# Expert biases of a mixture-of-experts layer: one-hot bias products on TensorE against rows loaded per block and copied into PSUM by VectorE

## The reference, cut to what matters

```
logits = x2d @ w_router + b_router
top_v, top_e = lax.top_k(logits, 4);  gates = softmax(top_v)
# the 2080 (token, expert) slots are sorted by expert and cut into blocks of one expert each
def expert_block(xb, e):
    hh = xb @ w_up[e] + b_up[e]                      # 2048 wide
    gate = minimum(hh[:, :1024], 7);  lin = clip(hh[:, 1024:], -7, 7)
    return (gate * sigmoid(1.702 * gate) * (lin + 1)) @ w_down[e] + b_down[e]
y[token] += gates * expert_block(...)
```

## Time and profile before

| | |
|---|---|
| median of the runs | 1387.74 us |
| span of the profiled execution | 1384.6 us |
| TensorE busy | 1333.6 us (96%) |
| VectorE busy | 927.2 us (67%) |
| ScalarE, GpSimd busy | 199.2 us, 108.2 us |
| DMA | 468.77 MB, mean 339 GB/s over the span |
| product groups of the loop | L1874 639.5 us, L1909 319.5 us |

### The profile page before, as it was taken

How to read it: one execution, slowest core, us unless ns; L and a number is a source line. 1 busy time by engine, 2 the same in 40 slices (tenths; PEclk the granted TensorE clock), 3 DMA queues, 4 the chain that set the end, 5 groups by cost and what they waited for, 6 DMA issues and landing times.

```text
span 1384.6 us, 22327 instructions
## 1 busy us (share of the span) xinstructions
PE 1333.6 (96%) x6750; PEld 546.0 (39%) x6750; DVE 927.2 (67%) x2107; ACT 199.2 (14%) x389; POOL 108.2 (8%) x152
## 2 busy tenths in 40 slices
PE   8999999988998999998999999899999998999997
PEld 7866565553332333332333333233333332333332
DVE  3525257655876777776687776677787775777778
ACT  4231133422010100100010100000010000000012
POOL 3000000000000001000100001000100000000100
PEclk9999989999999999999999999999999999999999
DMA  9505171055999999999999999999999999999995
GB/s 362 120 4 185 31 251 69 31 231 207 393 421 421 421 383 421 391 421 421 422 379 420 389 422 421 419 420 380 421 392 413 396 420 422 420 378 422 388 379 236
DMA packets 90653, 468.77 MB, mean 339 GB/s; under 512 B 11822, under 2 KB 28960, under 8 KB 40226
## 3 DMA queue, kind: packets, MB, share of 16 engines
q1 hardware_dynamic: 74318, 441.43, 78.8%
q0 software_dynamic: 7360, 16.79, 3.1%
q10 hardware_dynamic: 8948, 10.19, 2.1%
HBM read 623.60 MB, written 28.25 MB: 471 GB/s over the span
## 4 chain that ended last, share of the span: by engine, by line
PE 86%; DMA 9%; DVE 4%; issue 1%; ACT 0%; SPq 0%; DVEq 0%
PE ps L1874 42%; PE ps L1909 21%; DMA raw<-in_w_down_dram 8%; PE ps L1542 5%; PE ps L1565 5%; PE ps L1781 4%; PE ps L1844 2%; PE ps L1736 1%; PE ps L1735 1%; PE ps L1830 1%; PE ps L1520 1%; DVE v_gate L1481 0%; PE ps L1644 0%; PE ps L1727 0%; DVE v_gate L1475 0%
## 5 line engine op out<-in xcount | busy, mean ns | idle before, releaser
L1874 PE MATMUL ps<-raw,xT 128*64 128x512 f32 x2880 | 639.5, 594 | 14.3 <-DMA raw<-in_w_up_dram 14.1
L1874 PEld LDWEIGHTS ps<-raw,xT 128*64 128x64 f32 x2880 | 201.2, 137 | 388.6 <-issue 348.3
L1909 PE MATMUL ps<-raw,aT 128*64 128x512 f32 x1440 | 319.5, 593 | 7.9 <-DMA raw<-in_w_down_dram 7.9
L1370 DVE STREAM_TRANSPOSE xT<-x_hold 32x64 f32<-32x64 f32 (+1 forms) x704 | 282.5, 401 | 57.1 <-PE ps L1874 36.5
L1370 DVE STREAM_TRANSPOSE aT<-act_g 32x256 f32<-32x256 f32 x360 | 228.6, 635 | 54.6 <-PE ps L1909 44.4
L1909 PEld LDWEIGHTS ps<-raw,aT 128*64 128x64 f32 x1440 | 102.0, 137 | 210.1 <-issue 185.8
L874 ACT ACTIVATE act_s<-act_g 128x512 f32<-128x512 f32 x46 | 29.0, 630 | 714.2 <-DVE act_g L1354 714.1
L516 POOL DMA_INDIRECT slot_outputs<-y_rows,out_idx x44 | 44.4, 1010 | 603.4 <-ACT y_rows L879 603.4
L1276 DVE TENSOR_REDUCE found<-ps 128x2 f32<-128x8 f32 x48 | 8.0, 167 | 109.3 <-PE ps L1830 107.3
L508 POOL DMA_INDIRECT x_rows<-expert_inputs,row_idx x48 | 49.3, 1028 | 345.1 <-DVE row_idx L1277 209.7
L1781 PE MATMUL ps<-w_out_sb,mixT 128*128 128x512 f32 x128 | 56.8, 598 | 0.8 <-DVE mixT L1154 0.8
(11 more groups left out here) (368 smaller groups left out, 894.8 us busy)
## 6 DMA issues: line engine op xcount, KB each, us to landing
raw<-in_w_up_dram SPq DMA_DIRECT2D x368, 1024.0 KB
raw<-in_w_down_dram SPq DMA_DIRECT2D x184, 1024.0 KB
slot_outputs<-zeros ACTq DMA_DIRECT2D x1, 8320.0 KB, 28.1
raw<-slot_outputs SPq DMA_DIRECT2D x8, 1024.0 KB, 11.9
w_c_cols<-in_w_in_dram SPq DMA_DIRECT2D x1, 4096.0 KB, 32.0
w_out_sb<-in_w_out_dram SPq DMA_DIRECT2D x1, 4096.0 KB, 13.9
w_a_cols<-in_w_in_dram SPq DMA_DIRECT2D x1, 2624.0 KB, 13.0
x_sb<-in_x_prompt_dram SPq DMA_DIRECT2D x4, 512.0 KB, 5.3
```

The costliest lines, as they stand in the source:

```text
L1370: dve.transpose(dst_at(rows_out, group), src_at(rows_in, parity)).then_inc(done, 1)
L1874: ins = mm(ps[SUB * i:SUB * i + SUB, banks[bank], :], rows_in[:, j, :], raw[:, SLOT[j], c:c + HF], start=False, stop=(j == UPU - 1))
L1909: ins = mm(ps[SUB * i:SUB * i + SUB, 2, :], aT[:, j, r, :], raw[:, SLOT[UPU + j], D * r + HF * i:D * r + HF * i + HF], start=False, stop=( ...
```

## The change

The biases are no longer split and kept for all experts. Two small tiles hold the rows of one block's expert: `up_rows` [128, 2, 512] and `down_rows` [128, 512], of which only partitions 0 and 32 (half 0) and 64 and 96 (half 1) are loaded. ScalarE issues two loads for `up_rows` and two for `down_rows` in every turn of the loop, each into two partitions. VectorE copies the row in the first lane of each group of 32 partitions to all 32 with a shuffle, straight into the PSUM bank, for gate, lin and down; the products of the block then have no start flag and add to what stands there. TensorE's six bias products per block go, and so do both one-hot selects and the early preparation. Once per set of banks TensorE writes them with a dummy product (`mark_written`), so that later products accumulate.

```diff
-            for j in range(3):
-                sp.dma_start(b_stage[NE * j:NE * j + NE, 0:2 * FF], b_up[0]).then_inc(ld_biases, 16)
-                sp.dma_start(b_stage[NE * j:NE * j + NE, 2 * FF:3 * FF], b_down[0]).then_inc(ld_biases, 16)
...
+            act.wait_ge(w_a_cleared, 4)
+            for d in range(2):
+                act.dma_start(up_rows[32 * d:P:2 * 32], b_up[0, 0:1].rearrange("e (a i n) -> i (e a) n", a=2, i=2)).then_inc(ld_up_rows, 16)
+                act.dma_start(down_rows[32 * d:P:2 * 32], b_down[0, 0:1].rearrange("e (i n) -> i (e n)", i=2)).then_inc(ld_down_rows, 16)
...
+            def load_up_rows(b):
+                if not (isinstance(b, int) and b == 0):
+                    act.wait_ge(up_seeded, b)
+                src = b_up[0, column(expert(act, b))].rearrange("e (a i n) -> i (e a) n", a=2, i=2)
+                for d in range(2):
+                    act.dma_start(up_rows[32 * d:P:2 * 32], src).then_inc(ld_up_rows, 16)
+
+            def load_down_rows(b):
+                if not (isinstance(b, int) and b == 0):
+                    act.wait_ge(down_seeded, b)
+                src = b_down[0, column(expert(act, b))].rearrange("e (i n) -> i (e n)", i=2)
+                for d in range(2):
+                    act.dma_start(down_rows[32 * d:P:2 * 32], src).then_inc(ld_down_rows, 16)
...
             with act.Fori(1, nb) as b:
+                load_up_rows(b + 1)
                 sigmoid(b)
+                load_down_rows(b)
                 hold(b + 2)
                 y_out(b - 1)
...
-            dve.wait_ge(ld_biases, 6 * 16)
-            do(dve.tensor_copy(bias_parts[0:3 * NE, :], b_stage[:]))
-            do(dve.tensor_tensor(b_stage[:], b_stage[:], bias_parts[0:3 * NE, :], ALU.subtract))
...
+            def seed_up(b, banks):
+                dve.wait_ge(ld_up_rows, ROWS_LANDED * b + ROWS_LANDED)
+                dve.sem_inc(rows_seen, 1)
+                dve.stream_shuffle(ps[:, banks[0], :], up_rows[:, 0], FIRST_LANE)
+                dve.stream_shuffle(ps[:, banks[1], :], up_rows[:, 1], FIRST_LANE).then_inc(up_seeded, 1)
+
+            def seed_down(b):
+                dve.wait_ge(ld_down_rows, ROWS_LANDED * b + ROWS_LANDED)
+                dve.wait_ge(y_ready, b + 1)
+                dve.sem_inc(rows_seen, 1)
+                dve.stream_shuffle(ps[:, 2, :], down_rows[:], FIRST_LANE).then_inc(down_seeded, 1)
...
             indices(own, 0)
+            dve.wait_ge(banks_written, 1)
+            seed_up(0, FIRST_BANKS)
...
                 turn_a(b - 1, aT)
+                seed_down(b - 1)
                 indices(o, b + 2)
-                dve.wait_ge(up_bias_done, b + 1)
-                select(sel_up, b + 1, sel_up_ready)
...
                 clamp(b)
+                dve.wait_ge(up_read, b + 1)
+                seed_up(b + 1, (0, 1))
                 turn_x(b + 1, 1)
...
-                dve.wait_ge(dn_bias_done, b)
-                select(sel_dn, b, sel_dn_ready)
...
             def first_up():
                 for j in range(UPU):
+                    if j == 0:
+                        pe.wait_ge(up_seeded, 1)
...
+                    if j == 5:
+                        pe.wait_ge(table_made, 1)
+                        mark_written((0, 1, 2))
...
             def up(b):
-                pe.wait_ge(sel_up_ready, b + 1)
-                pe.wait_ge(up_read, b)
-                bias(0, 0, sel_up)
-                bias(1, FF, sel_up).then_inc(up_bias_done, 1)
+                pe.wait_ge(up_seeded, b + 1)
                 pe.wait_ge(xT_ready, 16 * b + 16)
...
             def down(b, aT, at_last=False):
 
-                pe.wait_ge(sel_dn_ready, b + 1)
-                pe.wait_ge(y_ready, b + 1)
-                bias(2, 2 * FF, sel_dn).then_inc(dn_bias_done, 1)
+                pe.wait_ge(down_seeded, b + 1)
```

More of the change, by code:

```diff
@@ L105, in moe_layer @@
         slots_row = keep("slots_row", [P, P])
-        bias_parts = keep("bias_parts", [P, 3 * D], BF16)
+        up_rows = keep("up_rows", [P, 2, HF])
+        down_rows = keep("down_rows", [P, HF])
         pos_table = keep("pos_table", [P, NTILE, NE])
@@ L335, in moe_layer @@
         xT_ready, x0_psum = sem("xT_ready"), sem("x0_psum")
-        sel_up_ready, sel_dn_ready, up_bias_done, dn_bias_done = (
-            sem("sel_up_ready"), sem("sel_dn_ready"), sem("up_bias_done"), sem("dn_bias_done"))
+        ld_up_rows, ld_down_rows = sem("ld_up_rows"), sem("ld_down_rows")
+        rows_seen, banks_written, up_seeded, down_seeded = (
+            sem("rows_seen"), sem("banks_written"), sem("up_seeded"), sem("down_seeded"))
         g_ready, up_read, sigm_ready, a_ready = sem("g_ready"), sem("up_read"), sem("sigm_ready"), sem("a_ready")
@@ L477, in _ @@
             made.do(pool.memset(gates[:], 0.0))
-            own.do(pool.memset(bias_parts[3 * NE:P, :], 0.0))
+            pool.memset(up_rows[:], 0.0).then_inc(w_a_cleared, 1)
+            pool.memset(down_rows[:], 0.0).then_inc(w_a_cleared, 1)
             pool.wait_ge(skew_written, 16)
@@ L882, in _ @@
             for b, dst in ((0, xT_first), (1, xT)):
+                if b:
+                    act.wait_ge(table_made, 1)
+                    load_up_rows(1)
                 for a in range(2):
@@ L1410, in _ @@
             find_slots(own, 3)
+            dve.wait_ge(banks_written, 2)
+            seed_up(1, (0, 1))
             dve.wait_ge(up_used, UPU)
@@ L1439, in _ @@
             turn_a(last - 1, aT)
+            seed_down(last - 1)
             dve.sem_inc(xT_ready, 16)
@@ L1446, in _ @@
             pick_outputs(last - 1)
-            dve.wait_ge(dn_bias_done, last)
-            select(sel_dn, last, sel_dn_ready)
             step, do, settle = own.step, own.do, own.settle
@@ L1454, in _ @@
                               ALU.mult).then_inc(small_made, 1)
+            seed_down(last)
+            dve.wait_ge(ld_up_rows, ROWS_LANDED * nb + ROWS_LANDED)
             dve.wait_ge(hitT_psum, 2)
@@ L1841, in _, with mark_written @@
             ins.then_inc(pos_psum, 1)
-            def bias(bank, c0, sel):
-                for i in range(2):
-                    ins = mm(ps[SUB * i:SUB * i + SUB, bank, :], sel[:], bias_parts[:, c0 + HF * i:c0 + HF * i + HF], start=True,
-                             stop=False)
-                return ins
+            def mark_written(banks):
+                everywhere = ones_b[:].unsqueeze(1).to_broadcast([P, HF // P, P])
+                for bank in banks:
+                    ins = mm(ps[:, bank, :], ones_b[:], everywhere, start=True, stop=True)
+                ins.then_inc(banks_written, 1)
             def turn_rows(b):
@@ L1855, in _ @@
             find(0)
+            mark_written(FIRST_BANKS)
             keep_busy(3)
@@ L1858, in _ @@
             mm(ps[:, 2, 0:NE], ones_f[0:NE, :], blocks_ahead[:], start=True, stop=True).then_inc(order_psum, 1)
-            pe.wait_ge(sel_up_ready, 1)
-            bias(FIRST_BANKS[0], 0, sel_up)
-            bias(FIRST_BANKS[1], FF, sel_up).then_inc(up_bias_done, 1)
             turn_rows(0)
@@ L1874, in up_unit @@
                         ins = mm(ps[SUB * i:SUB * i + SUB, banks[bank], :], rows_in[:, j, :],
-                                 raw[:, SLOT[j], c:c + HF], start=False, stop=(j == UPU - 1))
+                                 raw[:, SLOT[j], c:c + HF], start=False, stop=(j == UPU - 1), skip_group_check=True)
                 ins.then_inc(up_used, 1)
@@ L1910, in down @@
                                      raw[:, SLOT[UPU + j], D * r + HF * i:D * r + HF * i + HF], start=False,
-                                     stop=(j == DNU - 1 and r == 1))
+                                     stop=(j == DNU - 1 and r == 1), skip_group_check=True)
                     ins.then_inc(dn_used, 1)
```

38 lines of the change are left out of this document (8 added, 30 removed).

## The result

| | before | changed |
|---|---|---|
| median of 4 runs beside each other | 1389.45 us | 1402.22 us |
| span of the profiled execution | 1384.6 us | 1394.2 us (time 1395.96) |

The ratio on record is 1.0098, 95% interval 1.0075 to 1.0121 (the quotient of the two medians, 1.0092, lies inside it); run again beside two of the experiments it was 1.0087 (1.0060 to 1.0113). The forecast, 1401.5 us, was made against 1387.74. The profiled execution is the shortest of its four, so its rows understate the change: 9.6 us on the span, where the medians give 13.

A forecast was written before the change was run, and what follows sets the result against it. TensorE and the DMA engines were taken to bound the kernel in turns. +24.8 (two engines) -10 (dips) -2.5 (last window) +1.5 (start) = +13.8 us, a span of 1398.4; 3.1 for the median gave 1401.5 us, range 1384 to 1413.

The forecast's parts named there:

- TensorE's saving, limited by the idle time of the DMA engines, and the start of the expert stage: Expert stage: removing bias products saves at most DMA idle time, -10 and -2.5 us; a longer start adds +1.5 us.
- loads on two engines: Expert stage: each two-row bias load runs on two DMA engines, giving them 24.8 us more work (21 to 33).
- The engines are always the same: Bias loads on ScalarE's queue: the same two DMA engines carry every load, so the sum is +13.8 us.
- spread load: Rival on bias loads: engines differ from load to load, 3.1 us each, -1 to -12 us, 1381.5 us; chance 0.17.
- Idle time, -10 and -2.5: DMA engines in the expert stage: saving capped by idle time, -10 us in dips (3 to 16.7), -2.5 in the last window.
- TensorE alone decides: Rival in the expert stage: TensorE is the only bound, all 29 us of bias products are saved, 1360 us; chance 0.03.
- VectorE: Loop on VectorE: three shuffles per block at 0.69 us each, 0.48 us of cover left, so nothing shows.
- VectorE becomes the bound: Rival in the loop: shuffles of 1.10 us lengthen VectorE's chain, 1405 us; chance 0.05.
- Start, +1.5, and end, nothing: Expert stage start: two shuffles and dummy products add +1.5 us (0.5 to 2); end: one shuffle hidden, nothing added.
- the pause in the last window: Last window, where SyncE waits for a scatter following TensorE's progress: DMA idle time there gives -2.5 us.
- What would show it: Expert stage signs: DMA share about 0.97, TensorE's weight waits about 65 us, turns 20.96 us, shuffles 0.6 to 0.75 us.

The follow-up runs named there:

- experiment 1: Changed kernel without the blocks' bias loads, expert 0's rows serving every block; ratio 0.9901 to the kernel before.
- experiment 2: Changed kernel with each bias load of a block issued twice, the second time into lanes nothing reads; ratio 1.0294 to the kernel before.
- experiment 5: Changed kernel without the blocks' bias loads, plus one unread load per block of the same 24 KB into 16 partitions; ratio 0.9944 to the kernel before.
- experiment 9: Changed kernel with biases laid out once as a DRAM table, one load of 8 and one of 4 partitions per block; ratio 0.9995 to the kernel before.
- experiment 4: Changed kernel with the same two-row bias loads issued by GpSimd behind its gather instead of ScalarE; ratio 1.0083 to the kernel before.
- experiment 3: Kernel before with the same two-row loads added into unread memory, bias products staying on TensorE; ratio 1.0082 to the kernel before.

## Why the prediction was right, step by step

The steps can be put beside two differences: "rest of the change" is experiment 1 against before, "loads" is the changed kernel against experiment 1.

| step | forecast | measured |
|---|---|---|
| TensorE's saving, limited by the idle time of the DMA engines, and the start of the expert stage | -10 - 2.5 + 1.5 = -11 | -14 (0.9901) |
| loads on two engines | +24.8 (21 to 33) | +27 |
| sum | +13.8 | +13 (1.0093) |

The mechanism came as forecast; that the sum is off by only 1 us is in part luck. Its two terms are each off by 2 to 3 us in opposite directions, and the -10 was picked from between 3 and 16.7.

- *Loads on two engines.* The mechanism is shown by experiments 1, 2, 5 and 9 together with the landing times in experiment 5; the ratios alone leave a price per load open. In 464 to 485.6 us, the window of the earlier trace rows, the queues read:

```profile
q1 hardware_dynamic: 1242, 9.02, 100.0%
...
q10 hardware_dynamic: 20, 0.02, 0.3%
```

 20 packets per block, 12 runs and 8 completions, as counted. A run of 2 KB took 87 ns in the mean, not 92; six are 0.52 us, and with four completions of 10 ns on the same engine 0.56. The measured 0.60 is a little above both. A queue at 0.3% of 16 engines costs 2% of the kernel: the share of a queue says nothing on the fullest engine.
- *The engines are always the same.* This was the choice on which the sign hung, and spread load is out: experiment 5 shows what spreading would have given, and 1.0098 is not it. The Trainium skill ("DMA: Bandwidth & Descriptors", section "Why a DMA increments its semaphore by 16 and not by 1") names the lowest-numbered engines for this queue. The runs show that the load isn't spread; the numbers of the engines are in no row. By the same section GpSimd's queue would move from engine to engine, but the lag of the last two landings in experiment 4, 1.13 us, speaks against that for these loads, without settling it.
- *Idle time, -10 and -2.5.* The right size, since without the loads TensorE's 29 us were worth 14: the rival "TensorE alone decides" is out even then. With the loads there they are worth nothing: the changed kernel against experiment 3 is +1 us, nothing that can be told from zero. The products' removal and the loads are thus no two separate terms, and the forecast needed the first limited before the second was added.
- *VectorE.* The three shuffles took 0.69 us each:

```profile
719.35 0.70 DVE L1292 STREAM_SHUFFLE ps<-up_rows 128x512 f32<-128x512 f32 x1
719.96 0.69 DVE L1293 STREAM_SHUFFLE ps<-up_rows 128x512 f32<-128x512 f32 x1
```

 as taken from the one-input operation of the earlier trace rows and not from the transposes of the earlier trace rows; the cover was 0.51 us. Where it fell short, the price was small: 5 us for 0.95 us per turn. So the rival "VectorE becomes the bound" would have added about as little as it said.
- *Start, +1.5, and end, nothing.* From the first up product to the second sigmoid it takes 32.2 us before and 33.7 in both profiles of the changed kernel. So +1.5 us can be seen, but behind the first up product, where the forecast had only 0.64 - 0.43 of it. What came ahead of that product can't be told: it starts at 324.6 us in one execution of the changed kernel and 327.5 in the other, 327.0 before; the mixer ran at half the granted clock for 6.8 us near 194 in the first, 10.2 us before. The forecast had -2.5 for the pause in the last window and nothing for the end, but the end grew: from the last sigmoid to the end of the span there are 45.6 us before, 48.7 and 47.8 in the changed kernel, 48.5 without bias loads and 45.3 with the products put back. So these 2 to 3 us are there without any loads and go when the products are back (the loads added to the kernel before bring 1.5 us by themselves). The saving in the 44 turns is larger than the 14 us of the whole: 18.5 us, 979.7 against 961.2.
- *What would show it.* Turns of 20.96 us, q10 and the shuffles came as said. The DMA share did not fall to 0.97: it is 1.00 [against rows 4], and only the rate fell. The 8 KB packets took 320 ns in the mean instead of 317, and more of them (1026 against 672) over 400 ns, just after the dips, and this time counts as busy. Why they take longer is not shown. TensorE's waits were to be 65 us; the view lists 48.8. But 44 turns lasted 64.9 us more than 44 x 20.96, in the second profile 69.3. The view misses part of the wait; before, it lists 22.0 where the turns give 28.9.

## What to carry to other kernels

A small transfer beside a stream that is cut over all DMA engines costs what it puts on its fullest engine, about in full, as soon as that stream is near its limit; count the rows on that engine, not the bytes or the queue's share. Give it eight or sixteen rows (here by a table laid out once in idle time), and leave it out where the data are there already. Work taken from one engine is worth no more than the other bound leaves idle, so first cap the saving, then add what the change puts on that other bound.

## What the runs showed that I had not expected

- The lengths of the turns tell more than the view of waits: they split the 7.5 to 12 us of the loop into every third turn (+1.5 to +2.6 us) and the pairs of new experts (25.7 to 30 us).
- A delay of 0.95 us in nearly every turn of VectorE cost 5 us in all, since two bounds that take turns hide each other's waits.
- A load skipped by its condition costs little or nothing: leaving out 14 of 46 gave back 8 us of 27, 30%.
- A stretch of 6.8 us at half the clock cost about 1.6 us beside a full weight stream, too little for the ratio to tell; only the timelines of the last block show it.
- The landing times of the 16 parts of a weight unit show an overloaded pair of engines directly (the last two parts 1.6 us behind instead of 0.4), although no view of the profile names an engine.
